# The order and the queues of the first loads in a two-layer streaming-encoder trunk

## The chip, the cores and the metric

The kernel runs on one core of a Trainium2 chip. The metric is the device time of one execution in microseconds; a lower time is better. The inputs are float32, and every large product is made of three float32r passes over a high and a low part of each operand.

## The reference

Two layers over 512 tokens of width 2048, with a cross-attention into 256 memory tokens in each. What matters here is the very beginning: the memory is normalised and projected, and this is the first work that the kernel does.

```python
def reference(x, mem, mem_norm, w_mem_kv, ...):
    mem_n = rms_norm(mem, mem_norm)
    h = x
    for layer in range(DEPTH):                      # DEPTH = 2
        mem_k, mem_v = jnp.split(mem_n @ w_mem_kv[layer], 2, axis=-1)
        if layer < N_A_LAYERS:
            h = layer_a(h, ..., mem_k, mem_v)       # RG-LRU branch and memory branch
            ...
            k_sb, v_sb = jnp.split(rms_norm(h, kv_norm) @ w_kv, 2, axis=-1)
        else:
            h = layer_b(h, ..., k_sb, v_sb, mem_k, mem_v)   # stick-breaking attention and memory branch
    return rms_norm(h, final_norm)
```

`mem` is 256 x 2048, `w_mem_kv[layer]` is 2048 x 1024 and `mem_norm` has 2048 entries.

## The kernel before

The kernel is written engine by engine; every wait is a semaphore written by hand, and each engine runs its own list in order. The work is a sequence of groups G (one group is one product with 512 weight columns) of four slabs j each. A slab is four tiles k of 128 rows by 512 columns of weights. Slab (0, 0) is the first.

A slab goes through five hands:

1. SyncE issues the load of the slab's weights to `w_raw` (`load_slab`, L436). There are two buffers, and the load of slab j waits until VectorE has finished slab j - 2. The activations come through `f_raw` (`load_fill`, L443) in the same way.
2. ScalarE writes the high part, `w_hi` = weights times the norm gains (`gains`), one instruction per k (L741 in slab (0, 0), L658 later). It also writes the high part of the activations, `memt_hi`, which lies in `act_hi` (L737 one k at a time in slab (0, 0), L692 four at once later).
3. VectorE writes the low part `w_lo` (L1365 in slab (0, 0), L1253 later) and `memt_lo`, which lies in `act_lo` (L1362, later L1273).
4. TensorE waits for the low part of each k and makes three matmuls from it (L2015, L2016, L2017), first for one block of 128 memory tokens and then for the other. Slab (0, 0) has 24 matmuls: 12 that can start only as the k come, 12 that need nothing new.
5. The end of each slab frees its high part for ScalarE.

In slab (0, 0) ScalarE, for each k in turn, waits for the memory tile, writes `memt_hi`, waits (k = 0 only) for the gains, waits for the weight tile and writes `w_hi`. VectorE waits for the gains once, and then for each k writes `memt_lo` and `w_lo`. TensorE starts with nine warm-up matmuls (L2079) that need only constants.

Before slab (0, 0) the loads are issued on two queues. SyncE's queue (called q1 in the profile) gets weight tile 0, weight tile 1, memory tiles 1 to 3 in one transfer (L467), weight tiles 2 and 3 in one transfer (L468), then the memory tiles of slab (0, 1) (512 KB) and its weights (1024 KB), and the channel constants. ScalarE's queue (q10) gets memory tile 0 (L730) and then the gains (L731). A weight tile is 256 KB in 128 packets of 2 KB, a memory tile 128 KB in 128 packets of 1 KB, the gains are 32 KB in 128 packets.

Of the kernel before, what the change touches and what calls it, by code (L numbers as in the profile page):

```python
# [26 lines left out]
M = 256  # L27
# [81 lines left out]
def trunk(nc, x, x_t, mem, mem_t, gain_cols, chan_cols, w_mem_kv, w_in_a, w_rec_gate, w_in_gate,  # L109
# [4 lines left out]
    mem_tv = mem_t.rearrange("(c k p) t -> c p k t", k=4, p=P)  # L114
# [30 lines left out]
    with ExitStack() as ctx:  # L145
        def sb(name, shape, dt=F32):
            return ctx.enter_context(nc.sbuf_tensor(name, shape, dt))

        def sem(name):
            return ctx.enter_context(nc.semaphore(name))  # L150
# [6 lines left out]
        w_raw = sb("w_raw", [P, 2, KS, C])  # L157
        f_at = nc.sbuf_base
        f_raw = sb("f_raw", [P, 2, 4, C])
# [126 lines left out]
        gains = sb("gains", [P, 64])  # L286
# [24 lines left out]

        w_loaded = [sem("w_loaded0"), sem("w_loaded1")]
        f_loaded = [sem("f_loaded0"), sem("f_loaded1")]
        w_first = [sem("w_first0"), sem("w_first1")]
        f_first = sem("f_first")
        gains_loaded = sem("gains_loaded")
        chan_loaded = sem("chan_loaded")
# [111 lines left out]
        def _(sp):  # L429
# [32 lines left out]
                    group(G0 + q, in_column(q))  # L462

            w_0 = w_mem_kv[0, 0:C, 0:C].rearrange("(k p) n -> p k n", p=P)
            for k in range(2):
                sp.dma_start(w_raw[:, 0, k, :], w_0[:, k, :]).then_inc(w_first[k], 16)
            sp.dma_start(f_raw[:, 0, 1:4, 0:M], mem_tv[0, :, 1:4, :]).then_inc(f_loaded[0], 16)  # L467
            sp.dma_start(w_raw[:, 0, 2:4, :], w_0[:, 2:4, :]).then_inc(w_loaded[0], 16)  # L468
            for m in range(4):
                for j in range(4):  # L470
                    if m == 0 and j:
# [16 lines left out]
            def load_proj(s, u):  # L488
                b11, _, b21, b22, t1, t2, t3, t4 = weights(s, u // 14)
                if u < 14:  # L490
                    w, c = ((b11, 0), (b11, 1), (t3, 0), (t3, 1), (b21, 0), (t4, 0), (b21, 1), (t4, 1),
                            (t1, 0), (t1, 1), (t2, 0), (t2, 1), (b22, 0), (b22, 1))[u]
                else:
                    w, c = (t1, t3, b11, t2, b22, b21, t4)[(u - 14) // 2], u % 2
                if u < 6 or u >= 8:
                    sp.wait_ge(lo_ready, 4 * (U_PROJ[s] + u - (1 if u < 6 else 3)))
                sp.dma_start(proj_raw[RAW[u]], w[C * c:C * (c + 1), :].rearrange("(k p) n -> p k n", p=P)
                             ).then_inc(proj_loaded[RAW[u]], 16)
# [144 lines left out]
        def _(act):  # L643
# [83 lines left out]
                last.then_inc(kmt_read, 1)  # L727


            act.dma_start(f_raw[:, 0, 0, 0:M], mem_tv[0, :, 0, :]).then_inc(f_first, 16)  # L730
            act.dma_start(gains[:], gain_cols).then_inc(gains_loaded, 16)  # L731
            act.wait_ge(const_step, 5)
            nc.scalar.activation(nmx[:], ones[:, 0:4], ACT.Square)

            for k in range(KS):
                act.wait_ge(f_first if k == 0 else f_loaded[0], 16)
                nc.scalar.activation(memt_hi[:, k, :], f_raw[:, 0, k, 0:M], ACT.Copy).then_inc(fill_hi, 1)  # L737
                if k == 0:
                    act.wait_ge(gains_loaded, 16)
                act.wait_ge(w_first[k] if k < 2 else w_loaded[0], 16)  # L740
                nc.scalar.activation(w_hi[:, 0, k, :], w_raw[:, 0, k, :], ACT.Copy, scale=g_mem[:, k:k + 1]  # L741
                                     ).then_inc(hi_ready, 1)
            for m in range(4):
# [488 lines left out]
        def _(dve):  # L1232
# [610 lines left out]
            with dve.Fori(0, NPAIR) as i:  # L1843
                ch.enter(i, PER_B)
                for q in range(2):
                    G = 2 * i + (G_B + 1 + q)
                    for j in range(4):
# [9 lines left out]
                        if not second:  # L1857
                            for m, (t, _, _) in enumerate(Z_ORDER):
                                w = P * (t + 1)
                                dve.wait_ge(z_read, 4 * n + m + 1)  # L1860
                                k, b = keep[:, t, T - w:T], beta[:, t, T - w:T]

                                a1 = ch.mark(V.tensor_tensor(k[:, w - P:w], k[:, w - P:w], m_keep[:], ALU.max))
                                a2 = ch.mark(V.tensor_tensor(b[:, w - P:w], b[:, w - P:w], m_beta[:], ALU.mult))
                                ch.wait(a1)

                                a3 = ch.mark(V.tensor_tensor_scan(k[:, 1:w][:, ::-1], k[:, 1:w][:, ::-1],
                                                                  k[:, 1:w][:, ::-1], 1.0, ALU.mult, ALU.bypass))
                                ch.wait(a3)
                                V.tensor_tensor(b[:, 0:w - 1], b[:, 0:w - 1], k[:, 1:w], ALU.mult).then_inc(w_ready, 1)  # L1870
# [139 lines left out]
        def _(pe):  # L2010
# [44 lines left out]
            def h_transposed(q):  # L2055
                _, banks = h_unit(q)
                if q < 4:
                    pe.wait_ge(psum_read, 9)
                    pe.wait_ge(r_done, 2)
                    if q:  # L2060
                        pe.wait_ge(h_raw, q)
                else:
                    pe.wait_ge(r_done, 3)
                    pe.wait_ge(psum_read, 12 if H_UNITS[q][0] == 3 else 14)
                    if q > 5:
                        pe.wait_ge(h_raw, q - 1)
                for k in range(2):
                    for t in range(NT):
                        last = TE.transpose(banks[:, k, P * t:P * t + P], h_rows(q, t, k), ident[:])
                last.then_inc(h_tr, 1)  # L2070
# [347 lines left out]
```

## Time and profile before

| | |
|---|---|
| time, median of 3 runs | 1478.92 us (1478.85 to 1479.96) |
| time of the profiled execution | 1480.23 us |
| its span, first to last instruction | 1478.1 us |
| TensorE busy | 1462.5 us (99%) |
| TensorE weight loads busy | 1222.2 us (83%) |
| VectorE busy | 993.7 us (67%) |
| ScalarE busy | 715.5 us (48%) |
| GpSimd busy | 122.2 us (8%) |
| moved by DMA | 357.96 MB, mean 242 GB/s |

The time of a run is a little longer than the span, since it includes what lies around the first and the last instruction: here 1480.23 - 1478.1 = 2.1 us. Engines run beside each other, so their busy times don't add up. All times below are counted from the start of the span.

### The profile page before, as it was taken

Reading aid. Unit: us, or ns where it says so; the run is one execution under the profiler, and the core shown is the slowest. Engines: PE = TensorE matmul, PEld = TensorE weight load, DVE = VectorE, ACT = ScalarE, POOL = GpSimd, SP = SyncE. Lnnn points to the kernel's source line nnn. Section 1 sums busy time; section 2 is a strip of 40 time slices with the busy share of each in tenths; the row PEclk is TensorE's granted clock in tenths of the full one; section 3 lists DMA queues with packets and bytes.
Section 4 is the critical chain, followed back from the end, with each engine's and each line's share of the span. In section 5 each row is a group of like instructions: output and inputs, shape, how many; then the busy total and the mean of one; then the engine's idle time right before and its main releaser. Section 6 shows DMA issues by size and latency. Waiting matters only on the chain.

```text
span 1478.1 us, 18184 instructions
## 1 busy us (share of the span) xinstructions
PE 1462.5 (99%) x6850; PEld 1222.2 (83%) x6850; DVE 993.7 (67%) x1302; ACT 715.5 (48%) x1063; POOL 122.2 (8%) x184
## 2 busy tenths in 40 slices
PE   8999999999999999999999999999999999999997
PEld 7888888888888888888888888888888888888886
DVE  5764558465576896855569676566566556578877
ACT  5764454444544645663325654433433432455465
POOL 0001111111110000000010001110111111100000
PEclk9999999999999999999999999999999999999999
DMA  9696688787786997477999866677887878879853
GB/s 340 231 342 217 154 216 238 170 227 171 201 247 165 328 316 263 153 264 273 358 343 340 292 219 223 230 221 176 237 238 195 233 204 218 246 207 343 309 198 143
DMA packets 155261, 357.96 MB, mean 242 GB/s; under 512 B 7744, under 2 KB 25152, under 8 KB 151104
## 3 DMA queue, kind: packets, MB, share of 16 engines
q1 hardware_dynamic: 105040, 206.50, 40.2%
q0 software_dynamic: 29376, 102.77, 28.3%
q10 hardware_dynamic: 20784, 47.88, 9.0%
q8 instruction: 38, 0.62, 0.2%
q14 instruction: 23, 0.19, 0.0%
HBM read 310.98 MB, written 113.25 MB: 287 GB/s over the span
## 4 chain that ended last, share of the span: by engine, by line
PE 93%; DVE 4%; DMA 1%; ACT 1%; issue 0%; SPq 0%; ACTq 0%; DVEq 0%
PE main L2015 23%; PE main L2017 23%; PE main L2016 23%; PE aux L2015 5%; PE aux L2017 5%; PE aux L2016 5%; PE aux L2346 2%; PE aux L2290 1%; PE aux L2292 1%; PE aux L2288 1%; PE aux L2335 1%; PE main L2290 1%; PE main L2292 1%; PE main L2288 1%; DVE w_lo L1749 1%; DMA w_raw<-weight_sums 1%
## 5 line engine op out<-in xcount | busy, mean ns | idle before, releaser
L2015 PE MATMUL main<-act_hi,w_hi 128*128 128x512 f32 x1216 | 476.2, 392 | 0.0
L2017 PE MATMUL main<-act_hi,w_lo 128*128 128x512 f32 x1216 | 474.3, 390 | 0.0
L2016 PE MATMUL main<-act_lo,w_hi 128*128 128x512 f32 x1216 | 474.1, 390 | 0.0
L2017 PEld LDWEIGHTS main<-act_hi,w_lo 128*128 128x128 f32 x1216 | 228.4, 188 | 47.8
L2016 PEld LDWEIGHTS main<-act_lo,w_hi 128*128 128x128 f32 x1216 | 228.5, 188 | 46.5
L2015 PEld LDWEIGHTS main<-act_hi,w_hi 128*128 128x128 f32 x1216 | 228.5, 188 | 46.3
L1253 DVE SCALAR_TENSOR_TENSOR w_lo<-w_raw,gains,w_hi 128x512 fp32r<-128x512 f32 x188 | 128.8, 746 | 122.3 <-ACT w_hi L658 122.1
L658 ACT ACTIVATE w_hi<-w_raw,gains 128x512 fp32r<-128x512 f32 x188 | 120.6, 713 | 144.9 <-PE main L2017 116.3
L1245 DVE TENSOR_TENSOR w_lo<-w_raw,w_hi 128x1024 fp32r<-128x1024 f32 x88 | 104.1, 1222 | 93.9 <-ACT w_hi L653 93.7
L653 ACT ACTIVATE w_hi<-w_raw 128x1024 fp32r<-128x1024 f32 x88 | 88.4, 1056 | 152.3 <-issue 105.5
L2015 PE MATMUL main<-w_hi,act_hi 128*128 128x512 f32 x352 | 137.9, 392 | 1.6 <-DVE w_lo L1365 1.4
L2017 PE MATMUL main<-w_hi,act_lo 128*128 128x512 f32 x352 | 137.2, 390 | 0.0
L2016 PE MATMUL main<-w_lo,act_hi 128*128 128x512 f32 x352 | 137.2, 390 | 0.0
L1286 DVE TENSOR_TENSOR w_lo<-w_raw,w_hi 128x1024 fp32r<-128x1024 f32 x64 | 75.8, 1221 | 37.7 <-ACT w_hi L706 37.5
L706 ACT ACTIVATE w_hi<-w_raw 128x1024 fp32r<-128x1024 f32 x64 | 64.3, 1052 | 75.5 <-issue 59.3
L2015 PE MATMUL aux<-w_hi,act_hi 128*128 128x512 f32 x224 | 87.7, 392 | 0.8 <-DVE w_lo L1286 0.8
L2016 PE MATMUL aux<-w_lo,act_hi 128*128 128x512 f32 x224 | 87.3, 390 | 0.0
L2017 PE MATMUL aux<-w_hi,act_lo 128*128 128x512 f32 x224 | 87.3, 390 | 0.0
L2015 PEld LDWEIGHTS main<-w_hi,act_hi 128*128 128x128 f32 x352 | 66.1, 188 | 17.3 <-DVE w_lo L1365 2.9
L2017 PEld LDWEIGHTS main<-w_hi,act_lo 128*128 128x128 f32 x352 | 66.1, 188 | 13.8
L2016 PEld LDWEIGHTS main<-w_lo,act_hi 128*128 128x128 f32 x352 | 66.1, 188 | 13.3
L1036 ACT ACTIVATE w_hi<-w_raw 128x768 fp32r<-128x768 f32 x55 | 45.2, 841 | 58.5 <-PE main L2017 17.4
(300 smaller groups left out, 2039.0 us busy)
## 6 DMA issues: line engine op xcount, KB each, us to landing
w_raw<-in_w_in_a SPq DMA_DIRECT2D x32, 1024.0 KB, 7.4
w_raw<-in_w_in_b SPq DMA_DIRECT2D x32, 1024.0 KB, 6.7
weight_sums<-in_w_out_a POOLq DMA_DIRECT2D x48, 512.0 KB, 7.1
weight_sums<-in_w_out_b POOLq DMA_DIRECT2D x48, 512.0 KB, 7.9
w_raw<-weight_sums SPq DMA_DIRECT2D x18, 1024.0 KB, 7.8
weight_sums<-weight_sums POOLq DMA_DIRECT2D x32, 512.0 KB, 6.6
w_raw<-in_w_mem_kv SPq DMA_DIRECT2D x15, 1024.0 KB, 5.2
work<-weight_sums SPq DMA_DIRECT2D x14, 1024.0 KB, 7.4
```

Of the source, the lines that this page charges most:

```text
L653: nc.scalar.activation(w_hi[:, j % 2, k:k + 2, :], w_raw[:, j % 2, k:k + 2, :], ACT.Copy).then_inc(hi_ready, 2)
L658: nc.scalar.activation(w_hi[:, j % 2, k, :], w_raw[:, j % 2, k, :], ACT.Copy, scale=s).then_inc(hi_ready, 1)
L706: nc.scalar.activation(w_hi[:, u % 2, k:k + 2, :], proj_raw[RAW[u]][:, k:k + 2, :], ACT.Copy).then_inc(hi_ready, 2)
L1036: nc.scalar.activation(v_w[v_slot(n)][0], v_raw[v_slot(n)], ACT.Copy).then_inc(v_hi, 1)
L1245: V.tensor_tensor(w_lo[:, j % 2, k:k + 2, :], w_raw[:, j % 2, k:k + 2, :], w_hi[:, j % 2, k:k + 2, :].bitcast(F32), ALU.subtract).then_inc ...
L1253: V.scalar_tensor_tensor(lo, w_raw[:, j % 2, k, :], gain[:, KS * j + k:KS * j + k + 1], hi, ALU.mult, ALU.subtract).then_inc(lo_ready, 1)
L1286: V.tensor_tensor(w_lo[:, u % 2, k:k + 2, :], proj_raw[RAW[u]][:, k:k + 2, :], w_hi[:, u % 2, k:k + 2, :].bitcast(F32), ALU.subtract).then ...
L2015: TE.matmul(o, a[0], b[0], start=first, stop=False)
L2016: TE.matmul(o, a[0], b[1], start=False, stop=False)
L2017: return TE.matmul(o, a[1], b[0], start=False, stop=final)
L2288: TE.matmul(o, a_h, w_h[:, c], start=k == 0, stop=False)
L2290: TE.matmul(o, a_h, w_l[:, c], start=False, stop=False)
```

## The change

The first loads are issued in another order. SyncE's queue issues the four weight tiles of slab (0, 0) one by one, each with its own semaphore. Memory tiles 1 to 3, still one transfer of 384 KB, go to ScalarE's queue, which now issues the gains first, then memory tile 0, then tiles 1 to 3. No computation changes, the same bytes are moved, and the waits of the other engines stay as they are but for ScalarE's: it waits for each of the four weight tiles by itself, where k = 2 and k = 3 had waited for a common transfer.

```diff
-        w_first = [sem("w_first0"), sem("w_first1")]
+        w_first = [sem(f"w_first{k}") for k in range(3)]
...
             w_0 = w_mem_kv[0, 0:C, 0:C].rearrange("(k p) n -> p k n", p=P)
-            for k in range(2):
+            for k in range(3):
                 sp.dma_start(w_raw[:, 0, k, :], w_0[:, k, :]).then_inc(w_first[k], 16)
-            sp.dma_start(f_raw[:, 0, 1:4, 0:M], mem_tv[0, :, 1:4, :]).then_inc(f_loaded[0], 16)
-            sp.dma_start(w_raw[:, 0, 2:4, :], w_0[:, 2:4, :]).then_inc(w_loaded[0], 16)
+            sp.dma_start(w_raw[:, 0, 3, :], w_0[:, 3, :]).then_inc(w_loaded[0], 16)
...
+            act.dma_start(gains[:], gain_cols).then_inc(gains_loaded, 16)
             act.dma_start(f_raw[:, 0, 0, 0:M], mem_tv[0, :, 0, :]).then_inc(f_first, 16)
-            act.dma_start(gains[:], gain_cols).then_inc(gains_loaded, 16)
+            act.dma_start(f_raw[:, 0, 1:4, 0:M], mem_tv[0, :, 1:4, :]).then_inc(f_loaded[0], 16)
...
-                act.wait_ge(w_first[k] if k < 2 else w_loaded[0], 16)
+                act.wait_ge(w_first[k] if k < 3 else w_loaded[0], 16)
```

## Rows read from the trace of the kernel before

**Rows 1.** The page, busy time, share and instructions of TensorE.

```profile
PE 1462.5 (99%) x6850; PEld 1222.2 (83%) x6850; DVE 993.7 (67%) x1302; ACT 715.5 (48%) x1063; POOL 122.2 (8%) x184
```

**Rows 2.** Waits of TensorE: line, releaser, us in total, times, longest.

```profile
PE main L2288 <- DVE w_lo L1749: 1.9, 2, 1.2
PE main L2015 <- DVE w_lo L1365: 1.4, 2, 1.0
```

**Rows 3.** Chain of work, 0 to 12 us: start, us, what.

```profile
2.20 6.23 DMA w_raw<-in_w_mem_kv
...
10.02 0.50 PE main L2015
...
11.02 0.50 PE main L2015
```

**Rows 4.** Timeline from 0 us: start, duration, engine, line, operation.

```profile
0.81 0.43 ACTq L730 DMA_DIRECT2D f_raw<-in_mem_t  x1
...
1.27 0.45 ACTq L731 DMA_DIRECT2D gains<-in_gain_cols  x1
...
1.73 0.43 SPq L467 DMA_DIRECT2D f_raw<-in_mem_t  x1
...
3.05 0.20 ACT L733 ACTIVATE nmx<-ones 128x4 f32<-128x4 f32 x1
```

**Rows 5.** DMA issues, 0 to 14 us: count, KB, us from issue to landing.

```profile
w_raw<-in_w_mem_kv SPq DMA_DIRECT2D x1, 512.0 KB, 6.2
f_raw<-in_mem_t SPq DMA_DIRECT2D x1, 384.0 KB, 4.4
f_raw<-in_mem_t ACTq DMA_DIRECT2D x1, 128.0 KB, 3.5
...
gains<-in_gain_cols ACTq DMA_DIRECT2D x1, 32.0 KB, 3.8
```

**Rows 6.** DMA queues, 3.0 to 3.5 us: packets, MB, share of 16 engines.

```profile
q1 hardware_dynamic: 66, 0.12, 62.2%
q10 hardware_dynamic: 75, 0.07, 44.1%
```

**Rows 7.** DMA queues, 4.6 to 5.1 us (1 KB packets of L467).

```profile
q1 hardware_dynamic: 183, 0.19, 108.9%
```

**Rows 8.** DMA queues, 9.4 to 10.4 us (2 KB packets of weights).

```profile
q1 hardware_dynamic: 189, 0.39, 104.2%
```

**Rows 9.** DMA queues, 4.3 to 4.6 us (the gains on q10).

```profile
q10 hardware_dynamic: 52, 0.01, 17.8%
```

**Rows 10.** Timeline of ScalarE and VectorE in slab (0, 0), 6 to 11 us.

```profile
6.15 0.42 ACT L737 ACTIVATE act_hi<-f_raw 128x256 fp32r<-128x256 f32 x1 [0.30 <-DMA f_raw<-in_mem_t]
6.47 0.71 ACT L741 ACTIVATE w_hi<-w_raw,gains 128x512 fp32r<-128x512 f32 x1
...
7.21 0.75 DVE L1365 SCALAR_TENSOR_TENSOR w_lo<-w_raw,gains,w_hi 128x512 fp32r<-128x512 f32 x1 [0.19 <-ACT w_hi L741]
...
9.88 0.42 DVE L1362 TENSOR_TENSOR act_lo<-f_raw,act_hi 128x256 fp32r<-128x256 f32 x1
...
10.22 0.75 DVE L1365 SCALAR_TENSOR_TENSOR w_lo<-w_raw,gains,w_hi 128x512 fp32r<-128x512 f32 x1
```

**Rows 11.** Timeline at the starts of slabs (0, 1) and (0, 2).

```profile
13.42 2.74 DVE L1253 SCALAR_TENSOR_TENSOR w_lo<-w_raw,gains,w_hi 128x512 fp32r<-128x512 f32 x4 [1.02 <-ACT w_hi L658]
...
14.56 0.39 PE L2015 MATMUL main<-w_hi,act_hi 128*128 128x512 f32 x1
...
18.20 2.74 DVE L1253 SCALAR_TENSOR_TENSOR w_lo<-w_raw,gains,w_hi 128x512 fp32r<-128x512 f32 x4 [0.69 <-ACT w_hi L658]
...
20.00 0.39 PE L2015 MATMUL main<-w_hi,act_hi 128*128 128x512 f32 x1
```

**Rows 12.** Groups of instructions, 0 to 12 us: warm-up matmuls, busy us, mean ns.

```profile
L2079 PE MATMUL main<-ident,ones 128*128 128x128 f32 x18 | 4.2, 430 | 2.5 <-POOL m_beta L575 2.5
```

**Rows 13.** Line L2103, the same form of matmul later (min/median/max ns).

```profile
L2103 PE MATMUL aux<-work,ones x8: 272/275/276, 136.6 to 137.4; 128*128 128x128 f32 x8
```

## The prediction, made before the change was run

> **What bounds the kernel now.** I read the page first. TensorE is busy in 99% of the span [rows 1], so the end moves only if TensorE's work gets longer or shorter, or if its idle time does. The waits of TensorE say how much idle time there is: outside its first wait for constants, 1.4 us come before L2015 of slab (0, 0) and the largest other item, in the middle of the kernel, is 1.9 us [rows 2]. The change touches only loads that land in the first 9 us. So the question is when TensorE gets into its unbroken stream. The chain of waits for the first 12 us shows what sets that: the transfer of weight tiles 2 and 3 is issued at 2.20 and takes 6.23 us, so it lands at 8.43; then follow the high part, the low part and TensorE's third step at 10.02, and the fourth at 11.02 [rows 3]. From 11.02 on TensorE runs without a gap through the next slabs.
>
> I call a step k the three matmuls that wait for tile k. The time of step 3 is what everything behind it hangs on. It is 11.02 now.
>
> **A ceiling on both sides.** Slab (0, 0) can't cost more than its idle time: even if the whole 1.4 us of idling in it went away, the gain would be 0.1% of the time. So the change is worth something only in tenths of a microsecond, unless the new order makes a load much later.
>
> **Landings now, as a rule for landings after.** L730 is issued at 0.81 and lands 3.5 later, at 4.3, the gains at 1.27 + 3.8 = 5.07, L467 at 1.73 + 4.4 = 6.13 (ScalarE starts on it at 6.15), L468 at 8.43 [rows 3 to 5, 10]. How do two queues share the 16 DMA engines? While both had work, from 3.0 to 3.5, q1 moved 66 packets and q10 moved 75, although q1's are twice as large [rows 6]. So the queues take turns by packet, about one to one. The price of a packet on one engine, with all 16 busy: 16 x 0.5 / 183 = 0.044 us for 1 KB [rows 7], 16 x 1.0 / 189 = 0.085 us for 2 KB [rows 8], and 0.178 x 0.3 x 16 / 52 = 0.016 us for one of the gains [rows 9]. A tile is 8 packets per engine.
>
> With these I work out how much each engine must do before a transfer is over, and what is left as fixed lead and landing time. L730: 8 x (0.085 + 0.044) = 1.03, left 3.27. The gains: 16 weight packets, 8 memory packets, 8 of the gains = 1.36 + 0.35 + 0.13 = 1.84, left 3.23. L467: 16 weight packets, 32 memory packets, 8 of the gains = 1.36 + 1.41 + 0.13 = 2.90, left 3.23. Three transfers give nearly the same rest, so the rule holds. L468 gives 4.26 and a rest of 4.17: it lands almost 1 us later than the rule says. That is the other bound.
>
> **The change part by part.**
>
> *The gains first on ScalarE's queue.* They are over after 8 x (0.085 + 0.016) = 0.81, so they land at 0.81 + 3.25 = 4.1 instead of 5.07. Memory tile 0 now lies behind them and takes their place: 1.84 + 3.25 = 5.1 instead of 4.3. ScalarE needs the memory tile first and the gains 0.32 us later, so w_hi 0 starts at 5.1 + 0.32 = 5.4, where it was 5.13. That is a small loss of 0.3 us in step 0, and it is off the path: step 0 has no work waiting behind it until tile 1 is there. This part is worth nothing.
>
> *A third issue on ScalarE's queue.* It takes about 0.45 us, as the one before it [rows 4], and delays the table load and the first activation, which ended at 3.25, to 3.7. Memory tile 0 lands at 5.1, so 1.4 us cover it. Without that cover it would cost 0.45 us. SyncE issues as many transfers as before ahead of slab (0, 1), five, so these are issued at the same times; zero.
>
> *Weight tiles 2 and 3 one by one and without the memory tiles ahead.* By the rule tile 2 needs 24 weight, 16 memory packets and the gains: 2.04 + 0.70 + 0.13 = 2.87, landing at 6.1; tile 3 needs 32 and 24: 3.91, landing at 7.2. Both are far ahead of the 8.43 of now. This is the gain of the change: the wait for L468, 1 us before step 2 [rows 2], goes.
>
> *Memory tiles 1 to 3 on ScalarE's queue.* This is the cost, and what is late next. They are one transfer with one semaphore, so k = 1, 2 and 3 all wait until its last packet. Each engine has 8 + 8 + 24 = 40 packets on q10, and while these go, q1 gets 40 turns too: the 32 packets of all four weight tiles and 8 of slab (0, 1)'s memory tiles. The sum is 32 x 0.085 + 40 x 0.044 + 8 x 0.016 = 2.72 + 1.76 + 0.13 = 4.61. With the rest of 3.23 they land at 7.84; with the rest of L468 they land at 8.78. Now they land at 6.13. I take 7.84, since that rest was measured on the same transfer and two others, and keep 8.78 as the upper bound. The lower bound is 6.13, for the case that the turns are not taken as I read them.
>
> *From that landing to step 3.* Landing to activation 0.02, activation to w_hi 0.32, w_hi to w_lo 0.74 (6.15, 6.47, 7.21 [rows 10]). A w_lo to its step takes 0.80 (10.22 [rows 10], 11.02 [rows 3]). So step 1 comes 1.88 after the landing, at 9.72, where it was 8.02 (7.21 + 0.8). All weights are there, so VectorE then goes at its own pace, the 0.34 from act_lo to w_lo (9.88, 10.22 [rows 10]) and what remains of the 0.75 of w_lo, as it did from step 2 to step 3: 1.00 per k (10.02 to 11.02 [rows 3]). ScalarE has 0.32 + 0.71 per k with an overlap, so it keeps pace. Step 3 comes at 7.84 + 1.88 + 2.00 = 11.72, which is 3.88 after the landing and 0.70 us later than 11.02.
>
> *Is the shift covered behind it?* No: TensorE stands at every later start. Slab (0, 1) starts at 14.56 now, its first w_lo is ready at 13.42 + 0.75 = 14.17; slab (0, 2) starts at 20.00, its first w_lo is ready at 18.95 [rows 11]. Its loads are released by VectorE's end of slab (0, 0), so they shift by the same 0.70 and the slack of 1.05 stays. Later TensorE has few gaps [rows 2], and the work in front of these hangs on the ends of its own slabs. The shift is carried to the end.
>
> The Trainium skill, page "DMA: Bandwidth & Descriptors", sections "Queues, rings and completion order" and "Issuing engines are not separate DMA queues", says that each DMA engine goes round its queues by packets of about 9 to 17 descriptors, and that issuing from a second engine saves only the sequencer's issue time. On this the trace agrees: two queues share in equal turns [rows 6]. By the second rule alone, which speaks against any gain from the second queue, the result would be no change; it doesn't say that the shared turns make one transfer later.
>
> **The rivals.**
>
> *Early landing, a small gain.* If ScalarE's queue served the memory tiles no later than now (6.13), all weights would be in time, and step 3 would come at 6.13 + 3.88 = 10.01, 1.0 us earlier. But slab (0, 1) would then wait for its own w_lo at 14.17 instead of 14.56: its weights are behind the same bytes as before. So only the 0.39 us between the two are left, less 0.04 from a ready low part to its matmul: 0.35, 1478.6. For it speaks that the memory tiles are issued as early as now and that q10 got slightly more than half of the turns; against it the row of equal turns. It decides from a landing before 7.14, where step 3 is at 11.02.
>
> *The clock falls.* Warm-up matmuls take 430 ns on average [rows 12], and the same form later 275 ns [rows 13]; the step follows from TensorE having idled before the warm-up and worked through it. So the warm-up ran at the lower level (1.2 GHz) and the rest at the upper (2.4 GHz). After the change TensorE has nothing from the end of step 0 (about 5.4 + 0.74 + 0.80 + 1.0 = 7.95, a step lasting about 1.0 us, 10.02 to 11.02) to step 1 at 9.72: 1.8 us of idling where 1.0 us is the longest now, 2.7 us if the landing is 8.78. If that made the clock fall for as long as the warm-up's 4.2 us, half of it is lost, 2.1 us. With the late landing, 8.78 + 3.88 - 11.02 = 1.64, this is 3.7 us, 1482.7, slower than the bound below. It decides only if both happen, or if the lower level lasts over 4.5 us (half of it, with 0.70, is about 2.96). The idle 1.0 us of now didn't make the clock fall.
>
> The Trainium skill, page "TensorE: Matmul & The Clock Gate", section "HAM oscillation — how this bites in real kernels", has it that waits for data between bursts of matmuls bring the lower clock back. The trace of before shows no such fall; what it would make of the time is the rival above.
>
> *The shift is absorbed.* If one of the later waits hangs on something that TensorE's start doesn't move, such as GpSimd's transfers, part or all of the 0.70 us vanishes there, 1478.9. The 1.9 us of L2288 [rows 2] would be the place.
>
> **How the numbers follow.** Forecast 0.70, early landing 0.16, clock 0.05, absorbed 0.09. The profiled execution has 1480.23; by the sum it would be 1480.93. It lies 1.3 us above the median of the runs, and so I set the forecast by the median: 1478.92 + 0.70 = 1479.6. The likeliest case has 1478.9 to 1480.6 (landing 7.1 to 8.78). To this comes the scatter of the runs shown, 1.1 us, most of it upward. The range goes from 1478.2 (early landing, with 0.4 us of scatter) to 1481.1 (late landing, with 0.5). A measurement of this kernel can tell about 0.2%, 3.0 us, from no change. All cases but the clock's lie within it: faster 0.02, same 0.94, slower 0.04.
>
> **What would show it.** The gains' landing near 4.1 and memory tile 0 near 5.1; tiles 1 to 3 near 7.8; no ScalarE wait for weights in slab (0, 0); step 1 near 9.7, step 3 near 11.7; slab (0, 1) from 15.3; TensorE's wait before step 1 about 1.8 us and none before step 2. Wrong would be: step 3 before 11.0 (the turns are not equal), matmuls of 128x512 that take twice their 0.39 us after 9.7 us (the clock), or an end that doesn't move with step 3.

## The result and the profile after

The changed kernel takes 1483.56 us (median of 9 runs, 1481.26 to 1485.08) against 1479.96 us (9 runs, 1478.85 to 1480.78). The ratio is 1.0022, with a 95% interval of 1.0013 to 1.0030. By that ratio it is slower by 3.3 us (1.9 to 4.4), where 0.7 was forecast; the time lies 2.5 us above the range. The kernel before had been taken at 1478.92 us, the median of its first 3 runs; with 9 runs it is 1479.96, so 1.04 us of the 3.96 between the forecast 1479.6 and 1483.56 belong to that starting value and not to the change. The profiled execution took 1481.26 us with a span of 1479.1, which makes it the fastest of the nine and shows only part of the loss.

The page's busy times after (to [rows 1]) are those of before:

```profile
PE 1462.1 (99%) x6850; PEld 1221.5 (83%) x6850; DVE 993.9 (67%) x1302; ACT 715.3 (48%) x1063; POOL 122.5 (8%) x184
```

In the waits of TensorE after (to [rows 2]) the wait in slab (0, 0) has grown from 1.4 to 2.3 us, and its longest from 1.0 to 2.0:

```profile
PE main L2015 <- DVE w_lo L1365: 2.3, 2, 2.0
PE main L2288 <- DVE w_lo L1749: 1.9, 2, 1.2
```

The DMA issues after, 0 to 14 us, with the median time from issue to landing (to [rows 5]):

```profile
w_raw<-in_w_mem_kv SPq DMA_DIRECT2D x4, 256.0 KB, 4.3
f_raw<-in_mem_t ACTq DMA_DIRECT2D x1, 384.0 KB, 6.4
f_raw<-in_mem_t ACTq DMA_DIRECT2D x1, 128.0 KB, 3.9
...
gains<-in_gain_cols ACTq DMA_DIRECT2D x1, 32.0 KB, 3.3
```

The gains land at 0.81 + 3.3 = 4.1, memory tile 0 at 1.27 + 3.9 = 5.17, tiles 1 to 3 at 1.75 + 6.4 = 8.15; forecast were 4.1, 5.1 and 7.84. The timeline after, ScalarE, VectorE and TensorE from 8 us (to [rows 10] and [rows 11]):

```profile
8.16 0.42 ACT L737 ACTIVATE act_hi<-f_raw 128x256 fp32r<-128x256 f32 x1 [1.96 <-DMA f_raw<-in_mem_t]
...
10.03 0.50 PE L2015 MATMUL main<-w_hi,act_hi 128*128 128x512 f32 x1 [2.00 <-DVE w_lo L1365]
...
11.05 0.77 PE L2015 MATMUL main<-w_hi,act_hi 128*128 128x512 f32 x1
...
11.23 0.75 DVE L1365 SCALAR_TENSOR_TENSOR w_lo<-w_raw,gains,w_hi 128x512 fp32r<-128x512 f32 x1
...
12.47 0.63 PE L2015 MATMUL main<-w_hi,act_hi 128*128 128x512 f32 x1
12.90 0.63 PE L2016 MATMUL main<-w_lo,act_hi 128*128 128x512 f32 x1
...
16.61 0.39 PE L2015 MATMUL main<-w_hi,act_hi 128*128 128x512 f32 x1
```

Step 1 comes at 10.03 (9.72 forecast), step 2 at 11.05, where it was 10.02: 1.03 us late. So far it is the forecast with 0.3 us more on the landing. But then the matmuls follow each other every 0.43 us (12.47, 12.90) and show 0.63 us instead of 0.39. Step 3 starts at 12.47, although its low part was ready at 11.23 + 0.75 = 11.98, and slab (0, 1) starts at 16.61 instead of 14.56, 2.05 us late. The windows view has the reason in its PEclk column (the granted clock, third from the right end):

```profile
core 0: us, PE busy (x) PEld busy (x) DVE busy (x) ACT busy (x) POOL busy (x), PEclk, DMA share, GB/s
7.00:10.50 3.50, 1.46 (x5) 0.94 (x6) 1.70 (x4) 2.34 (x6) 0.00 (x0) 1.00 1.07 382
10.50:13.90 3.40, 3.40 (x10) 2.35 (x9) 3.29 (x6) 3.10 (x5) 0.00 (x0) 0.51 0.64 195
13.90:18.00 4.10, 4.10 (x20) 3.37 (x19) 3.29 (x5) 2.01 (x3) 0.00 (x0) 0.99 1.07 388
```

From 10.5 to 13.9 us the clock is at its lower level (1.2 GHz), though TensorE is busy there; ahead of it lie 2.0 us in which it had nothing to do. In the same stretch before the change TensorE made 16 matmuls at the upper level:

```profile
10.50:13.90 3.40, 3.37 (x16) 2.44 (x15) 2.17 (x3) 1.81 (x3) 0.00 (x0) 1.00 0.92 301
```

That is the rival called "the clock falls", which had 1 chance in 20.

### The profile page after: what moved, and what is told of

Its sections match the earlier page's. It is cut to its first block, busy times and chain, and to the rows that moved or that the text cites. A ratio compares the mean times of both kernels' runs of the same rounds, so it can differ in the third digit from the quotient of the medians.

```text
span 1479.1 us, 18185 instructions
## 1 busy us (share of the span) xinstructions
PE 1462.1 (99%) x6850; PEld 1221.5 (83%) x6850; DVE 993.9 (67%) x1302; ACT 715.3 (48%) x1063; POOL 122.5 (8%) x184
## 4 chain that ended last, share of the span: by engine, by line
PE 93%; DVE 4%; DMA 1%; ACT 1%; issue 0%; ACTq 0%; SPq 0%; DVEq 0%
PE main L2015 23%; PE main L2017 23%; PE main L2016 23%; PE aux L2015 5%; PE aux L2017 5%; PE aux L2016 5%; PE aux L2346 2%; PE aux L2288 1%; PE aux L2290 1%; PE aux L2292 1%; PE aux L2335 1%; PE main L2288 1%; PE main L2292 1%; PE main L2290 1%; DVE w_lo L1749 1%; DMA w_raw<-weight_sums 1%
## 5 line engine op out<-in xcount | busy, mean ns | idle before, releaser
L2017 PEld LDWEIGHTS main<-w_hi,act_lo 128*128 128x128 f32 x352 | 66.3, 188 | 13.9
```

The source lines that it names most:

```text
L2017: return TE.matmul(o, a[1], b[0], start=False, stop=final)
```

## The experiments

"Share low" is the number of runs with a mean granted clock of 0.997 or less; of the changed kernel's first nine runs eight were low. In the runs beside the experiments the kernel before had 10 of 108 such runs, unevenly spread: 1 of 35, 7 of 34, 2 of 21 and 0 of 18. Their median is 1483.5 us, that of the 98 others 1480.7. The landing is that of memory tiles 1 to 3 in the profile, "idle before step 1" is TensorE's wait there, "delay" is how much later slab (0, 1) starts than at 14.56, all in us. "hold2" and "hold3" are kernels in which only TensorE waits longer, "by need" is another order of the loads; they are explained below.

| kernel | landing | idle before step 1 | delay | share low | ratio (95%) |
|---|---|---|---|---|---|
| the kernel before again | 6.0 | 0.2 | 0.05 | 2 of 12 | 1.0004 (0.9995 to 1.0013) |
| the changed one again | 9.5 | 3.2 | 4.62 | 12 of 12 | 1.0021 (1.0011 to 1.0031) |
| the changed one, third profile | 8.55 | 2.4 | 2.14 | | |
| changed, matmuls in the gap | 10.3 | filled, then 2.0 | 3.16 | 1 of 11 | 1.0008 (1.0000 to 1.0017) |
| changed, memory tiles one by one | 7.2 (tile 1) | 0.9 | 0.74 | 7 of 12 | 1.0009 (1.0000 to 1.0018) |
| move only | 8.6 | 2.3 | 2.82 | 8 of 11 | 1.0014 (1.0005 to 1.0022) |
| split only | 6.2 | | -0.37 | 0 of 11 | 0.9996 (0.9986 to 1.0005) |
| gains only | 6.1 | | -0.12 | | |
| hold2 | 6.1 | 1.5 | 0.17 | 5 of 11 | 1.0009 (1.0000 to 1.0018) |
| hold2, filled | 6.3 | filled | 0.37 | 0 of 12 | 1.0006 (0.9997 to 1.0014) |
| hold3 | 6.0 | 3.0 | 2.86 | 8 of 8 | 1.0028 (1.0017 to 1.0038) |
| hold3, filled | 6.4 | filled | 1.66 | 0 of 11 | 1.0009 (1.0000 to 1.0018) |
| weights 2 and 3 held back | 5.95 | 0 (3.3 before slab (0, 1)) | 3.77 | 4 of 10 | 1.0025 (1.0015 to 1.0035) |
| by need | | | 0.41 | 0 of 11 | 0.9992 (0.9981 to 1.0003) |

**Both kernels again.** No edit.

> The kernel before, once more, for a second profile and for its clock in many runs. Both theories: time equal to the kernel before (ratio 1.000 within 0.05%). Clock theory: the mean granted clock is 0.998 to 0.999 in every run, since no idle time in slab (0, 0) is over 1.1 us and the clock never falls after the warm-up. Theory of the late landing plus chance: clocks may scatter down to 0.996 here too, since the fall would be chance and not caused by the idle time.

> The changed kernel once more, for a second profile. Both: 3 to 4 us over the kernel before (ratio 1.0022). Step 3 at 11.0 to 11.1 us in the profile, as in the first one. Clock theory: the clock falls again to 0.5 within some microseconds of TensorE's 2.0 us of idling, and the profile with the longer low stretch is the one with the longer span: at 1 us of delay at step 3, and half of the low stretch on top. Late landing alone: the delay at slab (0, 1) is 1.0 us whatever the clock does, and what is over that arises later in the kernel.

The second profile of the kernel before agrees with the first to 0.2 us at every step. The changed kernel is slower by the same ratio as at first, 1.0021, and all its 12 runs are low in clock. Its second profile has a later landing, TensorE idles 3.2 us and the lower level lasts twice as long, to 17.6. Its DMA issue (issue to landing 7.7):

```profile
f_raw<-in_mem_t ACTq DMA_DIRECT2D x1, 384.0 KB, 7.7
```

its wait of TensorE:

```profile
PE main L2015 <- DVE w_lo L1365: 3.5, 2, 3.2
```

and its windows, with a granted clock of about a half in both:

```profile
10.50:13.90 3.40, 2.52 (x6) 2.06 (x7) 3.22 (x6) 3.30 (x7) 0.00 (x0) 0.54 0.43 134
13.90:18.00 4.10, 4.10 (x11) 3.20 (x11) 3.42 (x6) 3.15 (x5) 0.00 (x0) 0.55 0.95 329
```

Slab (0, 1) starts, in its timeline, at 19.18:

```profile
19.18 0.39 PE L2015 MATMUL main<-w_hi,act_hi 128*128 128x512 f32 x1
```

> The changed kernel, one look, for a third profile. Memory tiles 1 to 3 land at 8 to 10 us, TensorE idles 2 to 4 us, the clock falls for 3.4 or 6.8 us, and the start of slab (0, 1) comes 2 to 4.6 us late. In the stage of seven value products, which takes 1.6 us less in two profiles of this kernel than in those of the kernel before: if that belongs to the kernel it is so here too (83.7 us for its 482 matmuls), if it is chance it may be 85.3 here.

The third profile (its timeline is below) has a landing at 1.75 + 6.8 = 8.55, 2.4 us of idling and the lower level again. So the clock fell in 3 profiles of 3, slab (0, 1) was late by 2.05, 4.62 and 2.14 us, 2.9 on average, and the runs say 3.1 to 3.3. The low part of k = 3 was ready 1.0, 2.4 and 1.4 us later than before the change (VectorE began it at 11.23, 12.57 and 11.63 instead of 10.22). So of the delays 1.6 us on average are the late landing, and the other 1.3 are what the lower level added (1.0, 2.3 and 0.7).

```profile
10.44 0.80 PE L2015 MATMUL main<-w_hi,act_hi 128*128 128x512 f32 x1 [2.44 <-DVE w_lo L1365]
11.03 0.63 PE L2016 MATMUL main<-w_lo,act_hi 128*128 128x512 f32 x1
```

**Matmuls in the gap.**

```diff
                         last = three_passes(o, a, b, kk == 0, kk == NK - 1)
+                        if form == "M" and t == 0 and G == 0 and j == 0 and k == 0:
+                            warm_up(8)
```

> The changed kernel with eight extra warm-up matmuls (about 1.8 us of work on constants, into a bank that nobody reads) between step 0 and step 1, so that TensorE idles 0.2 us instead of 2.0. Clock theory: the clock does not fall, the mean is 0.998 to 0.999, slab (0, 1) starts 1.0 us later than before, and the time is 1 us over the kernel before (ratio 1.0007), 2.3 us less than the changed kernel. Late landing plus something later in the kernel: the time stays 3.3 us over the kernel before.

The eight matmuls on constants take 2 us and add nothing to the result. Runs low in clock go from 12 of 12 to 1 of 11, and the ratio from 1.0021 to 1.0008. By these ratios about 1.9 us of the 3.1 hang on TensorE's idling, and 1.2 us are left for the late landing; the two intervals overlap a little, the counts of low runs don't leave a doubt. In the profile the memory tiles land later than in any other, at 1.75 + 8.5 = 10.25; even so, with 2.0 us of idling behind the fill, the granted clock stays at 1.00. The delay of 3.16 us in this profile is all late landing.

**Memory tiles one by one.** In the changed kernel tiles 1, 2 and 3 become three transfers on ScalarE's queue.

```diff
-            act.dma_start(f_raw[:, 0, 1:4, 0:M], mem_tv[0, :, 1:4, :]).then_inc(f_loaded[0], 16)
+            for k in (1, 2, 3):
+                act.dma_start(f_raw[:, 0, k, 0:M], mem_tv[0, :, k, :]).then_inc(f_rest[k], 16)
```

> The changed kernel with memory tiles 1, 2 and 3 as three transfers on ScalarE's queue, each with its own semaphore. If the queues take turns by packet, tile 1 needs 24 packets on each queue and lands near 6.5 us, tile 2 near 7.4, tile 3 near 8.2. Step 1 then comes at about 8.3, step 3 at about 10.4, and slab (0, 1) is held by its own weights at about 14.2 to 14.6. Clock theory: TensorE idles 0.3 us before step 1 as before the change, the clock does not fall, and the time is that of the kernel before or 0.3 us less (ratio 0.9998). If the fall of the clock is chance: the same step times, but a time 2 us over the kernel before.

Step 1 comes at 9.08 and step 3 at 11.74, each later than expected: tile 3 lands only at 9.88, later than the common transfer in the three profiles of the changed kernel. The time expected was that of the kernel before; the ratio is 1.0009 (1.0000 to 1.0018). Step 3 comes 0.72 us later than before and slab (0, 1) 0.74. Nor did the clock stay up as expected: the profile has no fall, with 0.9 us as its longest wait, yet 7 of 12 runs are low in clock. How long TensorE waited in those seven isn't known.

**The parts of the change alone.** Each is an edit of the kernel before. Move only:

```diff
-            sp.dma_start(f_raw[:, 0, 1:4, 0:M], mem_tv[0, :, 1:4, :]).then_inc(f_loaded[0], 16)
...
+            act.dma_start(f_raw[:, 0, 1:4, 0:M], mem_tv[0, :, 1:4, :]).then_inc(f_loaded[0], 16)
```

> The kernel before with one part of the change: memory tiles 1 to 3 go to ScalarE's queue, behind memory tile 0 and the gains; weight tiles 2 and 3 stay one transfer. If the shared turns of the queues are what makes the memory tiles late, they land at 8 to 10 us as in the changed kernel, TensorE idles 2 to 4 us before step 1, the clock falls, and the time is 3 us over the kernel before (ratio 1.002). If it is the new order of the gains or the splitting of the weights, the time here is that of the kernel before.

Split only:

```diff
-            sp.dma_start(w_raw[:, 0, 2:4, :], w_0[:, 2:4, :]).then_inc(w_loaded[0], 16)
+            sp.dma_start(w_raw[:, 0, 2, :], w_0[:, 2, :]).then_inc(w_first[2], 16)
+            sp.dma_start(w_raw[:, 0, 3, :], w_0[:, 3, :]).then_inc(w_loaded[0], 16)
```

> The kernel before with the other part: weight tiles 2 and 3 as two transfers with a semaphore each, still behind memory tiles 1 to 3 on SyncE's queue. Step 2 comes up to 0.6 us earlier, step 3 up to 0.3 us earlier or at the same time, slab (0, 1) starts at 14.2 to 14.6 us; TensorE's longest idle is at most 1.0 us and the clock does not fall. Time that of the kernel before (ratio 0.9995 to 1.0005). If the clock falls by chance whatever the loads do, some runs are at a mean clock of 0.996 here too.

Gains only:

```diff
+            act.dma_start(gains[:], gain_cols).then_inc(gains_loaded, 16)
             act.dma_start(f_raw[:, 0, 0, 0:M], mem_tv[0, :, 0, :]).then_inc(f_first, 16)
-            act.dma_start(gains[:], gain_cols).then_inc(gains_loaded, 16)
```

> The kernel before with the third part of the change alone: the gains ahead of memory tile 0 on ScalarE's queue. Memory tile 0 lands at 5.1 us instead of 4.3, the gains at 4.1, step 0 at 7.0 instead of 6.7, all else as before: step 1 at 8.0, step 3 at 11.0, slab (0, 1) at 14.6, no fall of the clock. Span within 0.3 us of 1478.1.

The move carries the loss. Alone it has the landing at 8.6, the idling and the low clocks; its ratio of 1.0014 has an interval that overlaps the whole change's. It had 8 low runs of 11, the kernel before 7 of 34 beside it. Its DMA issue and its wait of TensorE:

```profile
f_raw<-in_mem_t ACTq DMA_DIRECT2D x1, 384.0 KB, 6.9
```

```profile
PE main L2015 <- DVE w_lo L1365: 2.3, 1, 2.3
```

The order of the gains is free, as forecast. The split brings steps 2 and 3 0.85 us forward, more than expected, and then slab (0, 1) waits for its own weights until 14.19. The ceiling of 0.35 us in the prediction is here in the timeline of the split:

```profile
14.19 0.47 PE L2016 MATMUL main<-w_hi,act_hi 128*128 128x512 f32 x1 [0.30 <-DVE w_lo L1254]
```

**Weights 2 and 3 held back.** In the changed kernel SyncE waits for the memory tiles before weight tile 2.

```diff
             for k in range(3):
+                if k == 2:
+                    sp.wait_ge(f_loaded[0], 16)
                 sp.dma_start(w_raw[:, 0, k, :], w_0[:, k, :]).then_inc(w_first[k], 16)
```

> The changed kernel, but SyncE issues weight tiles 2 and 3 (and all that is behind them) only once memory tiles 1 to 3 have landed. If the shared turns with SyncE's transfers are what makes the memory tiles late, they land near 6.1 to 6.5 us, as before the change, and step 1 comes at 8.0 to 8.3; weight tile 2 then lands near 8.5 to 9, step 2 at about 10.5. If ScalarE's queue is slow by itself, or the larger number of packets ahead, the memory tiles land at 8 to 10 us here too.

Its DMA issue:

```profile
f_raw<-in_mem_t ACTq DMA_DIRECT2D x1, 384.0 KB, 4.2
```

The same transfer on the same queue lands 4.2 us after its issue, at 5.95, as soon as SyncE's queue has nothing behind weight tile 1. So it is not the queue but what shares the turns: by the prediction's rule the packets ahead are those of before, 2.90 + 3.23 = 6.13. The kernel as a whole is slow, since slab (0, 1)'s loads are issued only at 6.8 us and that slab waits 3.3 us:

```profile
18.33 0.47 PE L2017 MATMUL main<-w_hi,act_hi 128*128 128x512 f32 x1 [3.33 <-DVE w_lo L1255]
```

This wait says something on the clock as well. It is longer than any before step 1, and yet the clock stays up, in the wait and behind it:

```profile
14.60:18.30 3.70, 0.40 (x2) 0.00 (x1) 2.10 (x3) 2.06 (x4) 0.00 (x0) 1.00 0.99 351
18.30:22.00 3.70, 3.67 (x16) 3.09 (x17) 3.42 (x5) 2.97 (x5) 0.00 (x0) 1.00 0.59 179
```

Only 4 of 10 runs are low. Ahead of this wait TensorE had made matmuls from 10.24 to 15.0 with hardly a gap; in the profiles with a fall it had made the three of step 0 behind the warm-up. So the length of an idle stretch alone doesn't decide. The loss here is the late start: 3.77 us at slab (0, 1) against 3.7 by the ratio of 1.0025.

**Idling alone.** The loads are those of the kernel before; TensorE only waits longer before step 1, for the low part of k = 2 (hold2) or of k = 3 (hold3). The diff is that of hold3; hold2 has 3 in the place of the 4. In the filled forms it makes 8 or 14 matmuls on constants meanwhile.

```diff
-                            pe.wait_ge(lo_ready, 4 * (4 * G + j + extra[0]) + k + 1)
+                            pe.wait_ge(lo_ready, 4 if form == "M" and G == 0 and j == 0 and k == 1 else
+                                       4 * (4 * G + j + extra[0]) + k + 1)
```

> The kernel before, all loads as before, but TensorE waits before step 1 until the low part of k = 2 is ready, so that it idles about 2.3 us, from 7.7 to 10.0 us. Steps 1, 2 and 3 then follow at 10.0, 10.7 and 11.4. Without a fall of the clock slab (0, 1) starts 0.4 us later than before and the time is 0.4 us over the kernel before (ratio 1.0003). Clock theory: the clock falls as in the changed kernel, slab (0, 1) starts 2 to 4 us later, mean clock 0.996 to 0.997, time 2 to 3 us over the kernel before (ratio 1.0015 to 1.002). Then idling alone does it, with no load late.

> The kernel of hold2 with eight warm-up matmuls on constants (1.8 us) between step 0 and step 1, so that TensorE waits just as long for the same low part but idles only about 0.5 us of it. Clock theory: no fall, mean clock 0.998 to 0.999, slab (0, 1) 0.4 us later than before, ratio 1.0003. If the cost of hold2 came from the wait itself, it would be the same here.

> The kernel before, all loads as before, but TensorE waits before step 1 until the low parts of all four k are ready, at about 11.0 us, so that it idles 3.3 us, as long as in the profile of the changed kernel with the latest landing. Steps 1 to 3 then run back to back and slab (0, 1) starts about 1.1 to 1.4 us later than before if the clock stays up. Clock theory: it falls in the profile and in nearly all runs, mean clock 0.997 or less, slab (0, 1) starts 2.8 to 4.8 us late, ratio 1.002 to 1.003. If the fall has to do with the late loads or with the chip's state and not with idling: no fall, ratio 1.0008.

> The kernel of hold3 with fourteen warm-up matmuls on constants (3.1 us) between step 0 and step 1: the same wait for the same low part, but TensorE idles a few tenths of it. Clock theory: no fall, mean clock 0.998 to 0.999, slab (0, 1) starts 1.1 to 1.4 us late, ratio 1.0008. If the wait costs what hold3 costs in any case, the ratio is the same as there.

hold2 was inconclusive in its ratio: TensorE's recorded wait is 1.5 us where 2.3 was expected, its profile has no fall, and 5 of 11 runs are low in clock. These five have a median of 1482.72 us, the six others 1480.72, and none of the 12 runs of the filled form is low. hold3 decides. With no load late the clock falls in the profile and in 8 of 8 runs. The windows of hold3:

```profile
7.00:10.80 3.80, 0.99 (x3) 0.45 (x3) 2.69 (x6) 2.70 (x6) 0.00 (x0) 1.00 1.05 387
10.80:14.20 3.40, 3.19 (x8) 2.51 (x9) 2.21 (x4) 1.83 (x4) 0.00 (x0) 0.50 0.94 311
```

and of the filled form, which waits for the same low part:

```profile
7.00:10.80 3.80, 3.80 (x26) 3.52 (x26) 2.98 (x6) 3.11 (x6) 0.00 (x0) 1.00 1.06 389
10.80:14.20 3.40, 3.40 (x20) 2.87 (x20) 2.21 (x4) 1.83 (x4) 0.00 (x0) 1.00 0.93 319
```

The medians are 1484.23 and 1482.19 us: 2.0 us for the clock. In the two profiles slab (0, 1) is 1.2 us apart (delays of 2.86 and 1.66), and 0.3 us of the filled form's delay come from the fill, which ends behind the low part (step 1 at 11.31 instead of 11.01); so 1.5 us there. What the filled form still loses (1.0009) is the wait and these 0.3 us.

**By need.** A version meant to beat both: on SyncE's queue weight 0, then memory k and weight k in turn for k = 1, 2, 3.

```diff
+            sp.dma_start(w_raw[:, 0, 0, :], w_0[:, 0, :]).then_inc(w_first[0], 16)
+            for k in (1, 2, 3):
+                sp.dma_start(f_raw[:, 0, k, 0:M], mem_tv[0, :, k, :]).then_inc(f_rest[k], 16)
+                sp.dma_start(w_raw[:, 0, k, :], w_0[:, k, :]).then_inc(w_first[k] if k < 3 else w_loaded[0], 16)
```

> A version meant to beat both: seven transfers on SyncE's queue in the order in which ScalarE needs them (weight 0, memory 1, weight 1, memory 2, weight 2, memory 3, weight 3), memory tile 0 and then the gains on ScalarE's. From the packet prices memory 1 and weight 1 land near 5.4 to 5.9 us, memory 2 and weight 2 near 6.5 to 7.4, the last near 7.5 to 8.4. Steps 1, 2, 3 at 7.9, 8.9, 9.9 to 10.2; slab (0, 1) is held by its own weights at 14.2 (14.56 before), so the gain is 0.4 us and is carried to the end; no fall of the clock, mean 0.998 to 0.999. Ratio 0.9997, not to be told from 1 by the runs' times. If a late transfer of one DMA engine is the rule in any order, step 3 comes after 11 us.

Steps 1, 2 and 3 come at 7.33, 8.74 and 10.71, all earlier than before, step 3 by less than expected. But two issues more on SyncE's queue put slab (0, 1)'s weights later, and this slab starts at 14.97, 0.41 us late. By the end of the span its profile is 2.8 us behind the first profile of the kernel before. TensorE's waits for the weights of later slabs add up to 1.9 us in it (two waits, 0.2 us before), which is part of that; the rest wasn't followed up, and this profiled execution (1483.08 us) is slower than the median of its runs (1480.33). The runs (0.9992, interval from 0.9981 to 1.0003) can't tell it from the kernel before. So no version here is shown to beat the kernel before.

## Why the prediction was wrong, point by point

**Where it was right.** The bound (TensorE's stream, step 3); the worth of the gains' order (nothing); the earlier weights (no wait for them in slab (0, 0)); the cost of the moved memory tiles, which have to share turns with SyncE's queue (the kernel with weights 2 and 3 held back against the changed one); the ceiling of 0.35 us on a gain (0.37 in the profile of the split alone); and that a shift is carried on: in the first profile slab (0, 1) is 2.05 us late, and TensorE's matmuls at 800 us are late by the same 2.05.

**The first step that failed: the rest in the landing's sum.** The term "4.61 + 3.23 = 7.84, upper bound 8.78" was 8.15, 9.45 and 8.55 in three profiles of the changed kernel, 8.7 on average, and so 0.9 us more than forecast. If the 4.61 of shared turns is taken as it stands, the rest behind it was 3.54, 4.84 and 3.94 us, 4.1 on average. The prediction had this number in its own rows: L468, with the most packets to wait for (72 on each engine), had a rest of 4.17. It was kept as the bound, and 3.23 was taken from transfers with 16 to 56, where the moved memory tiles have 80. Even so the late landing alone, with its 1.64 us, would have stayed in the range.

What the longer rest is made of shows in part. In the second profile of the changed kernel q10 still moves a few packets of the memory tiles from 7.5 to 9.0 us, while q1 is far into the next slab's loads (its DMA queues in that stretch: packets, MB, share).

```profile
q1 hardware_dynamic: 467, 0.55, 100.3%
q10 hardware_dynamic: 44, 0.04, 8.0%
```

While both queues have work on an engine they move about as many packets each [rows 6]; here q10 moves a tenth of q1's, so most engines were done with the memory tiles and a few were not, and the landing, at 9.45, comes behind the last of them. Why single engines lag stays open; no run took it apart.

**The second step that failed: the clock was a rival with 0.05.** The prediction computed 1.8 to 2.7 us of idling and a price of 2.1 us, and both were right (2.0 to 3.2 us; 2.0 us from hold3 against its filled form). Wrong was the chance, argued from "the idle 1.0 us of now didn't make the clock fall". A row at 1.0 us says nothing of 2 or 3. So the sum had nothing for the clock, and this is the term that puts the result outside the range.

The runs give no length of idling at which the clock falls. Low in clock were 10 of 108 runs of the kernel before, 5 of 11 with 1.5 us of recorded wait before step 1 (hold2), 12 of 12 and 8 of 8 where the profiles show 2.0 to 3.2 us there; but only 4 of 10 with 3.3 us before slab (0, 1), behind almost five microseconds of matmuls. With 2 to 3.2 us before step 1, behind the three matmuls of step 0, the clock fell in 5 profiles of 5. Work ahead of the wait seems to keep the clock up, since the filled forms (0 or 1 low run each) point the same way; what decides it in a single run stays open.

Also the condition "it decides only if both happen" was met: late landing and fall come together, since the one makes the other. How long the lower level lasts was taken from the warm-up's 4.2 us; it lasted 3.4 us in the first profile and nearly 7 in the second. One reading behind the price stands on the durations alone: the profile's column has a granted clock of 1.00 during the warm-up too, although a warm-up matmul comes every 0.23 us there (18 in 4.2 us) and every 0.12 us in the fill of the gap (16 in 1.95 us), and the first matmuls of step 0 in hold2's profile take 0.80 and 0.63 us, as at the lower level later on. So the column doesn't show the lower level at the very start.

**The starting value.** The forecast was set on 1478.92, the median of three runs, and not on the profiled 1480.23. Nine runs have 1479.96, and the runs beside the experiments 1480.6 to 1480.8. From 1479.96 the range would have ended at 1482.1, still 1.4 us too low.

The Trainium skill, page "TensorE: Matmul & The Clock Gate", section "HAM oscillation — how this bites in real kernels", says that waits for data between bursts bring the lower clock back. Here the trace agrees, with a granted clock of 0.51 from 10.5 to 13.9 us behind a wait of 2.0 us; behind the wait of 3.3 us in the kernel with weights 2 and 3 held back it does not, with 1.00.

The Trainium skill, page "DMA: Bandwidth & Descriptors", section "Issuing engines are not separate DMA queues", says that issuing from several engines saves only the issue time. As a rule against a gain it held. It names no loss, and here there is one: the same bytes on a second queue landed 2.0 to 3.3 us later (6.13 against 8.15 to 9.45).

**What makes up the 3.3 us.** From the changed kernel against its filled form, 1.0021 - 1.0008, 1.9 us are the clock; from 1.0008, 1.2 us are the later start. Each ratio is known to about 0.1% either way, 1.5 us, so the split is rough. The three profiles show both parts but turn their sizes round: 1.6 us of late landing and 1.3 of clock on average. That both parts are there is shown, which is the larger is not.

## What to carry to other kernels

Putting a transfer on an emptier queue did not bring it forward: the two queues here took turns, and the small transfer that was needed now ran beside large ones that were needed later. When a load at the start of a kernel moves, count TensorE's idle time and not only its delay; here two to three microseconds of idling behind the warm-up and three matmuls cost 0.7 to 2.3 us more in clock in the profiles, and matmuls on constants in the gap took that part away. When rows of before give two values for one term, take the one measured under the conditions most like those after the change: the rest of 4.17 and not 3.23. A price that rests on one profiled execution should carry its spread: the same transfer landed at 8.15 and at 9.45 us.

## What else the runs showed

A stage in the middle of the kernel, the seven value products, runs at one of two paces. In the window from 815 to 890 us the kernel before made 427 matmuls:

```profile
815.00:890.00 75.00, 75.00 (x427) 65.14 (x426) 51.60 (x55) 45.41 (x55) 4.21 (x5) 1.00 0.79 256
```

the changed kernel 434 in its first profile (and 435 in its second):

```profile
815.00:890.00 75.00, 75.00 (x434) 65.57 (x433) 51.60 (x55) 46.23 (x56) 4.20 (x5) 1.00 0.79 264
```

and 427 again in its third:

```profile
815.00:890.00 75.00, 75.00 (x427) 64.97 (x425) 51.30 (x54) 44.90 (x54) 4.01 (x5) 1.00 0.79 256
```

7 of 427 are 1.6%, so 1.2 us over this window, at a granted clock of 1.00 in all. That is why the first profile of the changed kernel ends only 1.0 us late although it was 2.05 us late at 800 us. It comes and goes with the execution and explains part of the scatter. Of the 16 profiles four have the faster pace, all of them of the changed kernel or an edit of it (the other two are those with matmuls in the gap and with weights 2 and 3 held back); what sets it stays open. Single runs of the kernel before lie between 1478.0 and 1487.6 us, so they differ by more than the whole effect studied here, and this pace and the clock are two of the reasons.
